# Norm sums folded to 32 partitions on VectorE, three bf16 parts in one 96-row matmul

## What is computed

```
x = x + 1/2 * SwiGLU_1(RMSNorm(x))              # d_ff 2816
h = RMSNorm(x);  proj = h @ w_in                # latents, conv inputs, gates
A: latent attention, 8 heads of 96, causal      B: B * conv3(C * xc)
x = x + (sig(gA)*(A @ w_pa) + sig(gB)*(B @ w_pc)) @ w_out
x = x + 1/2 * SwiGLU_2(RMSNorm(x))

RMSNorm(x) = x * rsqrt(mean(x*x over the 1024 channels) + 1e-6) * gain
```

## Time and profile before

| | us |
|---|---|
| median of 3 runs | 3066.33 |
| lowest, highest | 3065.28, 3069.76 |
| the profiled execution's own time | 3066.17 |
| its span (slowest core, core 3) | 3064.6 |
| spans of all cores | 3055.1 to 3064.6 |
| PE busy in the span | 3040.6 |

### The profile page before, as it was taken

The page is one execution under the profiler, slowest core; times in us unless marked ns, Lnnn a source line. Parts: engine busy times, 40 slices in busy tenths (PEclk is TensorE's granted clock), DMA queues, the critical chain, the costliest instruction groups (busy, mean ns, idle before and its releaser), DMA issues.

```text
span 3064.6 us, 50030 instructions; the slowest of 8 cores (3055.1 to 3064.6 us)
## 1 busy us (share of the span) xinstructions
PE 3040.6 (99%) x16743; PEld 1435.3 (47%) x16743; DVE 1441.0 (47%) x2909; ACT 1301.0 (42%) x2015; POOL 384.1 (13%) x725
## 2 busy tenths in 40 slices
PE   8999999999999999999999999999999999999999
PEld 3444444544445444454444444444444454445544
DVE  4355554552545525455244552555425454254441
ACT  2244453631447314493143431446225572255730
POOL 1110110011100111001110011101111001110010
PEclk9999999999999999999999999999999999999999
DMA  9997998898987988859897998888987969878497
GB/s 171 165 153 127 149 148 155 142 168 138 151 165 124 158 143 146 157 95 165 145 158 140 161 165 142 137 166 143 168 142 130 182 113 169 143 129 157 84 160 146
DMA packets 122936, 451.87 MB, mean 147 GB/s; under 512 B 13888, under 2 KB 15040, under 8 KB 122560
## 3 DMA queue, kind: packets, MB, share of 16 engines
q0 software_dynamic: 103824, 414.82, 82.7%
q1 hardware_dynamic: 18864, 33.85, 3.7%
HBM read 846.62 MB, written 16.78 MB: 282 GB/s over the span
## 4 chain that ended last, share of the span: by engine, by line
PE 96%; DMA 3%; issue 0%; DVE 0%; ACT 0%; SPq 0%; POOL 0%; ACTq 0%; DVEq 0%; POOLq 0%
PE bank L655 39%; PE bank L728 20%; PE bank L985 10%; PE bank L964 7%; PE bank L1039 4%; PE bank L1157 4%; PE bank L1132 3%; DMA ring<-ws 3%; PE bank L756 2%; PE bank L1081 2%; PE bank L1143 2%; PE bank L821 1%; PE bank L825 1%; PE bank L816 0%; PE bank L619 0%; PE bank L906 0%
## 5 line engine op out<-in xcount | busy, mean ns | idle before, releaser
L655 PE MATMUL bank<-hT,ring 128*128 128x512 bf16 x4768 | 1049.6, 379 | 9.1 <-DMA ring<-ws 5.6
L655 PEld LDWEIGHTS bank<-hT,ring 128*128 128x128 bf16 x4768 | 463.9, 98 | 565.9 <-issue 17.0
L537 POOL DMA_DIRECT2D ring<-ws x720 | 383.4, 535 | 2654.1 <-PE bank L655 966.3
L728 PE MATMUL bank<-actT,ring 128*128 128x512 bf16 x2816 | 615.6, 379 | 0.0
L662 DVE TENSOR_TENSOR actT<-sg,bank 128x512 bf16<-128x512 f32 x340 | 233.5, 687 | 536.3 <-PE bank L655 400.6
L1043 ACT ACTIVATE actT<-bank,negM,par_sb 128x512 bf16<-128x512 f32 (+3 forms) x640 | 425.3, 727 | 134.5 <-PE bank L1039 92.9
L661 ACT ACTIVATE sg<-bank 128x512 f32<-128x512 f32 x340 | 203.2, 598 | 544.4 <-PE bank L655 485.8
L728 PEld LDWEIGHTS bank<-actT,ring 128*128 128x128 bf16 x2816 | 273.9, 98 | 324.8
L985 PE MATMUL bank<-hT,ring 128*128 128x512 bf16 x1344 | 379.4, 380 | 2.6 <-DMA ring<-ws 2.6
L731 DVE SCALAR_TENSOR_TENSOR xres<-bank,xres 128x512 f32<-128x512 f32 x128 | 88.5, 692 | 295.6 <-PE bank L728 294.9
L1039 PE MATMUL bank<-QT,KT 96*128 96x512 bf16 (+3 forms) x640 | 220.9, 349 | 0.0
(11 more groups left out here) (152 smaller groups left out, 2433.2 us busy)
## 6 DMA issues: line engine op xcount, KB each, us to landing
ring<-ws POOLq DMA_DIRECT2D x352, 512.0 KB, 8.5
ring<-ws POOLq DMA_DIRECT2D x128, 704.0 KB, 8.8
ring<-ws POOLq DMA_DIRECT2D x64, 896.0 KB, 10.9
ring<-ws POOLq DMA_DIRECT2D x64, 768.0 KB, 11.4
ring<-ws POOLq DMA_DIRECT2D x104, 256.0 KB, 10.3
xres<-x SPq DMA_DIRECT2D x64, 256.0 KB, 17.7
out<-xres SPq DMA_DIRECT2D x64, 256.0 KB, 10.1
uqkv<-ws POOLq DMA_DIRECT2D x1, 1088.0 KB, 18.6
```

The costliest lines, as they stand in the source:

```text
L537: [lambda e, off=off, wo_=wo_, F=F: e.dma_start(out=ring[:, off:off + F], in_=ws_d[:, wo_:wo_ + F])],
L655: op("pe", lambda e, k=k, a_=a_, wv=wv, pb=pb: e.matmul(pb[:], lhsT=wv[:, a_, k, :], rhs=h_[:, k, :], start=(k == 0), stop=(k == 7)), read ...
L728: op("pe", lambda e, kc=kc, wv=wv, ab=ab: e.matmul(ab[:], lhsT=wv[:, kc, :], rhs=actT[:, kc, :], start=(kc == 0), stop=(kc == NFC - 1)), r ...
```

## The change

The fp32 sums `acc` are first folded on DVE: `norm_fold` copies partitions 64 to 127 to a scratch on partitions 0 to 63 and adds them, then the same for 32 to 63. `norm_parts` splits the remaining 32 partitions into the three bf16 parts and puts them on partitions 0 to 31, 32 to 63 and 64 to 95 of one tile. `norm_finish` is one matmul over 96 rows. The fold is put one step ahead of the parts, except inside the mixers, where fold and parts stand together in the split's old place; for mixer norms the fold comes after the last down group of the FFN before. In the FFN norms of pool `AB` (the first two patterns) finish and applies move one step later.

```diff
     def norm_finish(pool):
         pb, dpb = psum(nbank[0] if pool is None else pool)
-        for i in range(3):
-            op("pe", lambda e, i=i: e.matmul(pb[:], lhsT=onesB[:], rhs=acc3[i], start=(i == 0), stop=(i == 2)),
-               reads=[d_onesB, d_acc3[i]], writes=[dpb], signal=(i == 2))
+        op("pe", lambda e: e.matmul(pb[:], lhsT=onesB[0:96, :], rhs=sqv[1][0:96, 0:512], start=True, stop=True),
+           reads=[d_onesB, d_sq[1]], writes=[dpb])
         rms_of(pb, dpb)
+
+    def norm_fold(ai=0):
+        acc, d_acc = accs[ai], d_accs[ai]
+        for n in (64, 32):
+            op("dve", lambda e, n=n: e.tensor_copy(out=sqb[0][0:n, :], in_=acc[n:2 * n, :]), reads=[d_acc], writes=[d_sq[0]])
+            op("dve", lambda e, n=n: e.tensor_tensor(out=acc[0:n, :], in0=acc[0:n, :], in1=sqb[0][0:n, :], op=ALU.add),
+               reads=[d_acc, d_sq[0]], writes=[d_acc])
+
+    def norm_parts(ai=0):
+        a, d_acc = accs[ai][0:32, :], d_accs[ai]
+        p3 = [sqv[1][32 * i:32 * i + 32, 0:512] for i in range(3)]
+        q2 = sqv[0][0:32, 0:512]
+        op("dve", lambda e: e.tensor_copy(out=p3[0], in_=a), reads=[d_acc], writes=[d_sq[1]])
+        op("dve", lambda e: e.tensor_tensor(out=a, in0=a, in1=p3[0], op=ALU.subtract), reads=[d_acc, d_sq[1]], writes=[d_acc])
+        op("dve", lambda e: e.tensor_copy(out=q2, in_=a), reads=[d_acc], writes=[d_sq[0]])
+        op("dve", lambda e: e.tensor_tensor(out=p3[2], in0=a, in1=q2, op=ALU.subtract), reads=[d_acc, d_sq[0]], writes=[d_sq[1]])
+        op("dve", lambda e: e.tensor_copy(out=p3[1], in_=q2), reads=[d_sq[0]], writes=[d_sq[1]])
...
         if norm:
-            sc[0] = [L(norm_split, 1)]
+            sc[0] = [L(norm_parts, 1)]
             sc[1] = [L(norm_finish, (4, 5))]
...
-        sc[n] = sc.get(n, []) + [norm_split]
-        sc[n + 1] = [L(norm_finish, pool)]
+        if pool is None:
+            sc[n] = sc.get(n, []) + [norm_fold, norm_parts]
+            n -= 1
+        else:
+            sc[n] = sc.get(n, []) + [norm_fold]
+            sc[n + 1] = [norm_parts]
+        sc[n + 2] = [L(norm_finish, pool)]
         for c in range(8):
-            sc[n + 2 + c // 2] = sc.get(n + 2 + c // 2, []) + [L(norm_apply, xb, hb, gcol, c)]
+            sc[n + 3 + c // 2] = sc.get(n + 3 + c // 2, []) + [L(norm_apply, xb, hb, gcol, c)]
...
                 if g + 1 < ng:
-                    sm_[0] = [L(norm_split, 1)]
+                    sm_[0] = [L(norm_fold, 1), L(norm_parts, 1)]
                     sm_[1] = [L(norm_finish, None)]
...
         if kind == "f1":
+            if (nk, ng_) == ("f1", 1) or nk == "f2":
+                sched[NFC + 7] = sched.get(NFC + 7, []) + [L(norm_fold, 1)]
             ffn(xb, hb, "f1", sched, stats_after=True, cold=cold)
```

## The result

The changed kernel is slower: it took 3087.21 and 3084.82 us, the ratio to the kernel before is 1.0066 (95% interval 1.005 to 1.0082), where 3084 us, a ratio of 1.0058, was forecast. The profiled execution took 3087.21 us, its slowest core is core 7.

The account below looks back on a forecast made before the run. TensorE, busy 99%, was taken to bound the kernel, with each added wait paid in full. 3066.2 - 9.1 (matmuls) + 25.5 (stalls) + 1.7 (clock fall) = 3084.3, predicted as 3084 us, range 3074 to 3099.

Parts of the forecast that it names:

- The saving: On TensorE's path, 63 norm matmuls become 21; 42 at a pitch of 0.216 us take away 9.1 us.
- The unseen fold copies: The fold's two fp32 copies on VectorE, in no row before, were priced at 0.42 us; the dear end was 0.685.
- rival (a): VectorE instructions on 64 and 32 partitions are quicker, so its chain stays within its room: faster, 3057 us; chance 9%.
- (c): The fold's copies cost 0.685 us instead of 0.42, with more clock falls: slower still, 3091 to 3104 us; chance 20%.
- The last copy: VectorE's bf16 copy to partitions 32 to 63, the parts' fifth step: between 0.21 and 0.42 us, 0.29 taken.
- The chain against its room: Before the norm matmuls, TensorE stalls where VectorE's fold and parts exceed the time available: 25.5 us in sum.
- the first mixer's norm: First of six FFN norms taken inside a mixer: 0.2 us more room, so 0.2 less than the 1.35 us stall.
- the seventh norm of the first pattern: Mixer norm in the first such FFN stage: matmul ready at 148.68 instead of 148.44, a stall of 0.2 us.
- The order on VectorE: At the second FFN's start chunk 0's gating product queues behind the fold, delaying the parts: stall 1.88 us, six times.
- The clock: TensorE falls to half clock once, after the first mixer's 3.1 us stall: 1.7 us; none after 1.88 us stalls.
- Waits for weights: TensorE's waits for weight transfers might shrink because stalls give the transfers time: at most 5 us back.
- rival (b): Nearly no change, 3061 to 3071 us: steps cost four fifths of their price, or weight waits shrink; chance 7%.

Follow-up runs that it names:

- one-matmul kernel: The kernel before with one norm matmul per norm in place of three, after all of the split, nothing folded: 3055.7 to 3058.0 us, ratio 0.9981.
- the kernel before with the later places: The kernel before, split and three matmuls as they were, with norm matmuls (all but the first) and applies one step later: 3066.4 and 3068.0 us.

## Why the prediction was right

The forecast was right in its mechanism: TensorE waits before 19 norm matmuls for VectorE's longer chain, by the amounts forecast for each pattern, and the version with the matmuls later shows that this is the loss.

- **The saving.** 42 matmuls at 0.216 us are 9.1 us. The one-matmul kernel shows 5.8 us with 1.9 us of new stalls in it, so 7.7 of the 9.1, with an interval of 3.5 us to either side that holds the forecast.
- **The unseen fold copies**, the widest bound: 0.42 us as the row of the cast said, not the 0.685 of the copy out of PSUM, by the groups of the changed kernel:

```profile
L625 DVE COPY sq<-acc 64x512 f32<-64x512 f32 x21 | 9.1, 433 | 1.2
L635 DVE CAST sq<-acc 32x512 bf16<-32x512 f32 x21 | 8.7, 415 | 2.2
L626 DVE TENSOR_TENSOR acc<-acc,sq 32x512 f32<-32x512 f32 x21 | 14.3, 680 | 2.2
L637 DVE COPY sq<-sq 32x512 bf16<-32x512 bf16 x21 | 6.3, 301 | 2.2
```

  The add takes 0.680 us on 32 partitions, 0.69 on 128 (L581), so a fourth of the partitions saves 0.01 us per step. With it rival (a), cheap instructions on few partitions, is out, and so is (c), whose copies were to take 0.685. The forecast's reason was weaker than the result: the row that it rested on has 1024 bf16 elements beside 512 fp32 ones, so the two do not differ in partitions alone. The last copy took 0.30 us, 0.29 was chosen.
- **The chain against its room**, pattern by pattern: total 26.4 us against 25.5. The largest miss of one pattern is 1.57 instead of 1.35 us in the mixers:

```profile
1008.76 0.69 DVE L1166 TENSOR_TENSOR QT<-actT 128x512 bf16<-128x512 f32 x1
1009.48 0.42 DVE L625 COPY sq<-acc 64x512 f32<-64x512 f32 x1
```

  The fold's first copy starts 0.72 us after the independent instruction before it started, where the split started 0.61 after it. The last copy took 0.36 us there instead of 0.29, and TensorE started 0.25 us after it instead of 0.15; the other steps gave 0.06 back. The Trainium skill (VectorE: DVE Perf Modes, section Two Vector instructions with no wait between them) has the rule, used in the forecast, that a start in another group of 32 partitions holds the instruction until the earlier ones are done. The trace agrees: this copy, which reads from partition 64 on, starts 0.03 us after the end of the one before it. The price was 0.11 us, below the 0.18 us estimated. Why TensorE started later here is open. Two small terms were off: the first mixer's norm was forecast 0.2 us cheaper and cost 1.59 us like the others, and the seventh norm of the first pattern was forecast to wait 0.2 us and did not wait on core 7.
- **The order on VectorE.** That the fold ahead of the gating product delays it and the parts by the queue was forecast and seen (product at 775.48 behind the add at 774.87). It is still the better of the two places tried: behind the product the stall is 3.2 to 3.6 instead of 1.8 us.
- **The clock** is the part that was right by luck. One fall of 1.7 us was counted behind the 3.1 us stall. It came on three of the eight cores in the changed kernel's profile, on five in its second one, and not on the slowest core of the first. Matmuls and stalls give 17.3 us, the measured difference is 20 to 22, and the rest is clock spells elsewhere, in part at a level of 0.81 that the forecast did not have. As assumed, no fall came behind the idle times of 1.64 us, at any of the six places on any core. But the forecast's reason, that 2.25 us of lost time had no fall and 2.6 had, does not hold: on the changed kernel's core 7 a wait for weights of 2.09 us, which ended at 145.2, was followed by the stretch at half clock at 146.5, and on the kernel before's core 7 one of 2.65 us at 1694.2 was followed by none. The length alone does not decide it.
- **Waits for weights** did not shrink: they are 15.2 us on core 7 of the changed kernel and 14.3 on core 7 of the kernel before, 12.8 and 13.0 in the mean of all cores. The largest line of each, the kernel before first:

```profile
PE bank L655 <- DMA ring<-ws: 9.5, 5, 3.6
PE bank L671 <- DMA ring<-ws: 9.7, 4, 3.9
```

  With that and with the prices of the steps, both halves of rival (b) are out.

## What to carry to other kernels

The busy share of an engine (VectorE 47%) does not say whether work can be added to it. The distance between the end of its chain and the start of the instruction that needs it does, and where that margin is 0.04 us, as at the second FFN's start, each added step is paid in full unless it can be hidden earlier. A change that trades TensorE's instructions for a longer chain elsewhere has to move the consumer as well: with the matmul one step later, the same work on VectorE turned a loss of 0.66% into a gain of 0.23%, each against runs of the kernel before beside it. Folding over partitions did not make the later steps on VectorE shorter: at 512 elements along the row they took 0.68 and 0.41 us on 32 partitions, 0.69 and 0.42 on 128.

## What the hardware showed that was not expected

TensorE's granted clock has a level of 0.81 that comes for 4 to 15 us at a time, at about the same time on two neighbouring cores or more, and without idle time before it (on core 7 of the changed kernel TensorE is busy all through 388 to 407.5 us). It came in the one-matmul kernel and in the kernel before with the later places too, and not in the profile of the kernel before. What brings it on is open.

The fall to half behind idle times near 3 us is not the same on all cores. Behind the same idle time of 2.96 us it came on 3, 5 and 5 of 8 cores in three profiles, and on all of cores 0 to 3 in a fourth. Behind 1.64 us it came in none of 48 cases in either profile of the changed kernel, and behind 3.1 to 3.4 us in 37 of 50. So idle time of TensorE is not priced by its length alone: six idle times of 3.1 to 3.4 us instead of 1.64, with a seventh added, cost 20 us, of which 11 to 13 are stalls.
